# Two blocks on one core: the second block's first projections read their inputs before the norm, and its factor is applied at the eviction

## The chip, the cores and the metric

One NeuronCore of one Trainium2 chip runs the whole program in one launch. The metric is the device time in microseconds, given as the median of the runs. Five engines work in parallel, each through its own list of instructions, and wait for each other by semaphores: PE (TensorE: matmuls), ACT (ScalarE), DVE (VectorE), POOL (GpSimd) and SP (which only starts DMAs here).

## The reference, cut to what matters

Two transformer blocks follow one another on 512 tokens of width 1024. Block one has two layers and ends in a gated convolution MLP, a residual addition and an RMS norm with the gain `final_g`. Block two has two layers as well; each begins like this:

```
x = rms_norm(x_lat, final_g)                  # end of block one
for l in range(2):                            # block two
    h = rmsnorm(x, norm_mix_g[l])             # x * rsqrt(mean(x*x) + 1e-6) * g
    proj = h @ w_in[l]                        # 7328 columns, among them
    c_q, c_kv, k_pe, sb_q, sb_k, sb_v, r_q, r_k, r_v, r_g, gate_logits = split(proj)
    q  = rmsnorm(c_q, mla_q_norm_g[l])  @ mla_w_uq[l]
    kv = rmsnorm(c_kv, mla_kv_norm_g[l]) @ mla_w_ukv[l]
    ... three attention branches, gates, output projection ...
    x = x + square(relu(rmsnorm(x, norm_mlp_g[l]) @ w_up[l])) @ w_down[l]
```

The factor of an RMS norm is one number for each token. It commutes with a matmul over the width: `(x * g * s) @ W = ((x * g) @ W) * s`. "Latents" below are `c_q` (384 columns), `c_kv` (256) and `k_pe` (32); "values" are `sb_v` (512).

## The kernel before

**Layout.** Activations lie with the width on the 128 partitions: `X[:, k, 256:768]` (`lat(X, k)`) is slice k of 8 of the 512 tokens. The first 256 columns of each slice hold context rows in block one and are free later. Every weight is streamed in chunks; a chunk goes by DMA into one of three `raw` slots, ACT makes the rounded half `whi` of it (line 1392), DVE the rest `wlo` (line 2141), and PE multiplies three times for each slice: high by high, high by low, low by high (`lin`, line 608; `lin_pair`, line 647, alternates two chunks slice by slice; `lin_tok`, line 666, puts tokens on the partitions of the result). ACT and DVE split ahead by `LOOK` = 2 chunks, and a slot of `whi` or `wlo` comes free when PE has finished the chunk three before. An activation that feeds such a matmul is split in the same way, on ACT (`nh`) and DVE (`nl`); PE waits slice by slice for `nl`.

**Order.** All orders are written out by hand: each engine has one program (`pe_program`, `act_program`, and so on), and a wait holds up all that stands behind it on that engine. `Line.wait_ge` names events, `fence` names the place that all four engines have passed.

**The end of block one.** `conv_ffn(1, ...)` ends in eight output slices `ct`, each a chunk of 1024 rows and one of 384. DVE adds each to `X` (line 2432). `with_stats` squares the new slice on ACT (line 1443), POOL adds the squares of slices 0 to 6 (line 2919), and PE sums over the partitions with a matrix of ones in fp32 (lines 695 and 687, PSUM bank 6). Beside it a generator, `tables()`, makes the sine and cosine tables of block two, one step for each of the eight slices: the second table's sines come at the last slice. Then `in_place("fin1", ...)` scales all of `X` by the factor and `final_g` (lines 1826, 1828, 2612); ACT squares the eight new slices and PE sums them (lines 1101 to 1104); ACT makes the second factor (1416, 1419), DVE multiplies by gain and factor (2171), ACT and DVE split (1426, 2163), and the first pair of `w_in_2` starts. In the second layer of block two the same norm stands between the last `w_down_2` slice (additions in lines 2888 and 2890) and the pair, with the one sum that the MLP's slices have gathered.

**The latents and values.** P0 to P5 below are the six latent chunks of `w_in_2` (P0 and P1 are the pair, P5 holds `k_pe` four times), P6 to P9 the four chunks of the values (`lin_tok`, line 678). ACT evicts each latent (`evac_c`, line 1847) into `CQ` or `KR`; its squares are summed for the inner norms of `c_q` (after P3, bank 6) and `c_kv` (after P5, bank 7). The inner norm of `c_q` is made on ACT and DVE between P4 and P5, that of `c_kv` after P5. ACT evicts the values (line 1871). Later projections of `w_in_2` read the same `BH` and `BL`, first near the end of the MLA attention (`n` = 16).

**The model for the change that is already there.** The MLP of block two works in the way that the change gives to the latents: `u_high` and `u_low` (lines 2082 and 2863) split `x * norm_mlp` before the factor is known, beside the output projection; the pair of `w_up_2` follows at once, and the two sums come after it.

Of the kernel before, what the change touches and what calls it, by code (L numbers as in the profile page):

```python
# [307 lines left out]
def build(nc, A, out):  # L308
# [187 lines left out]
    POSI = at("posi", [128, TL], I32, oA)  # L496
    POSF, ANG, KKt, RR = ring("rt", 4, oA + 2 * KB)
    PRS = at("prs", [128, TL], F32, oT)[:, :]
    W = oR
    BNORM = (ring("brs", 1, W + 18 * KB), ring("btr", 3, W + 20 * KB))  # L500
# [52 lines left out]
    MLA_ITEMS = [(j, i) for j in range(4) for i in range(4)]  # L553

# [37 lines left out]
    def pe_program(q):  # L592
# [399 lines left out]
        def conv_ffn(i, segs, side, fill):  # L992
# [8 lines left out]
            for half in range(2):  # L1001
# [21 lines left out]
                if half:  # L1023
                    beside(fill)
                    with_stats(S, out_ct, True if i == 0 else None)
# [85 lines left out]
        for l in range(2):  # L1111
            q.note(f"end_mlp{l}", "pe")
            br = lambda k: [("nl", f"b{l}", k)]
# [14 lines left out]
            lin_tok("w_in_2", B, br, 4, TOK4)  # L1128
# [230 lines left out]
            for half in range(2):  # L1359
                for jj in range(16):  # L1360
# [5 lines left out]
                    lin("w_up_2", B, ur, ONE)  # L1366

# [3 lines left out]
                if half:  # L1371
                    with_stats(f"mlp{l}", down)
# [8 lines left out]
    def act_program(q):  # L1381
# [75 lines left out]
        def with_stats(S, step, ctx=False, high=None):  # L1457
# [10 lines left out]
            stats_square(S, 7, 7, srcs(7))  # L1468

# [207 lines left out]
        def conv_ffn(i, segs, mixer, side, fill):  # L1677
# [27 lines left out]
            for half in range(2):  # L1705
# [11 lines left out]
                def out_ct(ct):  # L1717
                    chunk("ffn_w_out")
                    chunk("ffn_w_out")
                    if half:  # L1720
                        next(side, None)

                if half:
                    with_stats(f"ffn{i}", out_ct, i == 0)
# [106 lines left out]
        in_place("fin1", "ffn1", fence("end_block1"))  # L1831
        for k in range(8):
            square("x2", k, 0, lat(X, k), k % 2, *sq_by[k % 2], ("x", "x2", k))
            sq_by[k % 2] = [("sqmm", "x2", k, 0)]

        for l in range(2):
            q.note(f"end_mlp{l}", "act")
            f = fence(f"end_mlp{l}")
            for _ in norm_high(f"b{l}", "mlp0" if l else "x2", 0, 8, lambda k: BH[:, k, :], BNORM, f, rbank=6 if l else 7):
                pass  # L1840
# [4 lines left out]
            def evac_c(i, ct):  # L1845
                q.wait_ge(("mm", i), *f)
                e.activation(CQ[:, ct, :] if ct < 5 else KR, PS[plan[i][6][0]], ACT.Copy).then_inc(q.did("ev", i, 0))
                q.note("cq", l, ct)

            pair = [chunk("w_in_2", n) for n in range(2)]  # L1850
            for ct, i in enumerate(pair):
                evac_c(i, ct)
            stats_square(f"q{l}", 0, 2, [(CQ[:, 0, :], [("cq", l, 0)])])
            for ct in range(2, 6):
                evac_c(chunk("w_in_2"), ct)
# [10 lines left out]
            f2 = fence(f"end_latent{l}")  # L1866
            for g in range(4):
                i = chunk("w_in_2")
            for ti, b in enumerate(plan[i][6]):
                q.wait_ge(("mm", i), *f)  # L1870
                e.activation(sv(ti), PS[b].rearrange("p (a k) -> p a k", a=2), ACT.Copy).then_inc(q.did("ev", i, ti))
                q.note("sv", l, ti)

# [54 lines left out]
            for n in range(16 + 4):  # L1928
# [185 lines left out]
            for half in range(2):  # L2114
# [3 lines left out]
                def down(ct):  # L2118
                    chunk("w_down_2")
                    chunk("w_down_2")  # L2120

                if half:
                    with_stats(f"mlp{l}", down)
# [8 lines left out]
    def dve_program(q):  # L2132
# [310 lines left out]

        def conv_ffn(i, segs, mixer, side, fill):
# [36 lines left out]
            for half in range(2):  # L2483
# [14 lines left out]
                for ct in range(8):  # L2498
# [4 lines left out]
                    if half:  # L2503
                        next(side, None)
                    else:
                        beside(fill, 2)
            if i == 0:
# [107 lines left out]
        in_place("fin1", "x2", "final_g")  # L2615
# [12 lines left out]
        for l in range(2):  # L2628
            q.note(f"end_mlp{l}", "dve")
            f = fence(f"end_mlp{l}")  # L2630
            for _ in norm_low(f"b{l}", None, 8, lambda k: (lat(X, k), []), lambda k: col("norm_mix", 8 * l + k),
# [611 lines left out]
```

## Time and profile before

| what | us |
|---|---|
| median of 3 runs | 3837.73 (3837.13 to 3845.9) |
| profiled execution, its own time | 3840.83 |
| span of its profile | 3839.0 |
| PE busy | 3713.3 (97%) |
| DVE busy | 1594.2 (42%) |
| ACT busy | 1389.4 (36%) |
| POOL busy | 243.1 (6%) |

Busy time says how long an engine worked, not whether anything waited for it. The span runs from the first to the last recorded instruction; 1.83 us of the execution lie around it. PE's mean granted clock was 0.988 of full speed.

### The profile page before, as it was taken

Reading aid. Unit: us, or ns where it says so; the run is one execution under the profiler, and the core shown is the slowest. Engines: PE = TensorE matmul, PEld = TensorE weight load, DVE = VectorE, ACT = ScalarE, POOL = GpSimd, SP = SyncE. Lnnn points to the kernel's source line nnn. Section 1 sums busy time; section 2 is a strip of 40 time slices with the busy share of each in tenths; the row PEclk is TensorE's granted clock in tenths of the full one; section 3 lists DMA queues with packets and bytes.
Section 4 is the critical chain, followed back from the end, with each engine's and each line's share of the span. In section 5 each row is a group of like instructions: output and inputs, shape, how many; then the busy total and the mean of one; then the engine's idle time right before and its main releaser. Section 6 shows DMA issues by size and latency. Waiting matters only on the chain.

```text
span 3839.0 us, 45566 instructions
## 1 busy us (share of the span) xinstructions
PE 3713.3 (97%) x19200; PEld 2998.7 (78%) x19200; DVE 1594.2 (42%) x2532; ACT 1389.4 (36%) x2265; POOL 243.1 (6%) x199
## 2 busy tenths in 40 slices
PE   7998899999999999999899999999999999999998
PEld 6887778888887977888676768888877676888887
DVE  3217635423434155545445443433334544343333
ACT  3235523212224155323346442342324544234232
POOL 1000010000000001000000001110110001112011
PEclk9999999999999999999999999999999999999999
DMA  6320122333312222233211123322221122332322
GB/s 231 110 83 2 37 74 89 115 122 126 113 62 87 66 67 75 94 94 95 89 57 50 66 74 100 102 93 99 96 90 57 56 72 69 97 104 93 99 94 83
DMA packets 108701, 333.98 MB, mean 87 GB/s; under 512 B 11472, under 2 KB 26704, under 8 KB 108368
## 3 DMA queue, kind: packets, MB, share of 16 engines
q1 hardware_dynamic: 108496, 331.06, 26.7%
q8 instruction: 151, 2.47, 0.3%
q14 instruction: 54, 0.44, 0.0%
HBM read 327.35 MB, written 2.10 MB: 86 GB/s over the span
## 4 chain that ended last, share of the span: by engine, by line
PE 93%; DVE 4%; ACT 2%; issue 1%; DMA 0%; POOL 0%; SPq 0%; DVEq 0%; ACTq 0%
PE ps L625 69%; PE ps L678 6%; PE ps L661 2%; PE ps L726 1%; PE ps L1230 1%; PE ps L880 1%; PE ps L1078 1%; PE ps L1066 1%; PE ps L1057 1%; PE ps L687 1%; PE ps L907 1%; PE ps L1233 1%; PE ps L1109 1%; PE ps L1274 1%; PE ps L1151 1%
## 5 line engine op out<-in xcount | busy, mean ns | idle before, releaser
L2141 DVE TENSOR_TENSOR wlo<-raw,whi 128x1024 fp32r<-128x1024 f32 (+3 forms) x547 | 618.6, 1132 | 887.3 <-ACT whi L1392 886.9
L1392 ACT ACTIVATE whi<-raw 128x1024 fp32r<-128x1024 f32 (+3 forms) x547 | 526.3, 964 | 795.8 <-PE ps L625 624.9
L625 PE MATMUL ps<-bh,whi 128*128 128x512 f32 x1248 | 494.8, 397 | 0.1
L625 PE MATMUL ps<-bh,wlo 128*128 128x512 f32 x1248 | 486.1, 389 | 0.0
L625 PE MATMUL ps<-bl,whi 128*128 128x512 f32 x1248 | 485.9, 389 | 0.0
L625 PE MATMUL ps<-ah,whi 128*128 128x512 f32 (+2 forms) x1424 | 423.3, 356 | 0.2 <-ACT gv L1537 0.2
L625 PE MATMUL ps<-al,whi 128*128 128x512 f32 (+2 forms) x1424 | 417.8, 352 | 0.0
L625 PE MATMUL ps<-ah,wlo 128*128 128x512 f32 (+2 forms) x1424 | 415.0, 350 | 0.0
L625 PEld LDWEIGHTS ps<-ah,whi 128*128 128x128 f32 x1424 | 240.0, 188 | 51.1 <-issue 18.3
L625 PEld LDWEIGHTS ps<-bh,whi 128*128 128x128 f32 x1248 | 234.3, 188 | 58.1 <-issue 7.6
L625 PEld LDWEIGHTS ps<-bl,whi 128*128 128x128 f32 x1248 | 234.4, 188 | 50.2 <-issue 2.9
L625 PEld LDWEIGHTS ps<-bh,wlo 128*128 128x128 f32 x1248 | 234.2, 188 | 49.5
L625 PEld LDWEIGHTS ps<-ah,wlo 128*128 128x128 f32 x1424 | 242.1, 188 | 31.7
L625 PEld LDWEIGHTS ps<-al,whi 128*128 128x128 f32 x1424 | 241.2, 188 | 29.3
L625 PE MATMUL ps<-uh,wlo 128*128 128x512 f32 x512 | 199.2, 389 | 0.0
L625 PE MATMUL ps<-uh,whi 128*128 128x512 f32 x512 | 199.2, 389 | 0.0
L625 PE MATMUL ps<-ul,whi 128*128 128x512 f32 x512 | 199.2, 389 | 0.0
L2919 POOL TENSOR_TENSOR sq<-sq,sq 128x512 f32<-128x512 f32 x50 | 77.1, 1542 | 1908.8 <-ACT sq L1443 1908.8
L2881 DVE TENSOR_TENSOR ul<-rl,uh 128x512 fp32r<-128x512 f32 x64 | 44.3, 692 | 204.3 <-ACT uh L2098 204.3
L625 PEld LDWEIGHTS ps<-uh,whi 128*128 128x128 f32 x512 | 96.1, 188 | 20.0
L625 PEld LDWEIGHTS ps<-ul,whi 128*128 128x128 f32 x512 | 96.1, 188 | 19.9
L625 PEld LDWEIGHTS ps<-uh,wlo 128*128 128x128 f32 x512 | 96.1, 188 | 19.9
(367 smaller groups left out, 5947.4 us busy)
## 6 DMA issues: line engine op xcount, KB each, us to landing
raw<-weights_d SPq DMA_DIRECT2D x447, 512.0 KB, 3.4
aw<-ada_d SPq DMA_DIRECT2D x96, 512.0 KB, 3.8
raw<-weights_d SPq DMA_DIRECT2D x48, 256.0 KB, 2.6
raw<-weights_d SPq DMA_DIRECT2D x44, 192.0 KB, 2.3
x<-nab_d SPq DMA_DIRECT2D x24, 256.0 KB, 2.8
x<-x_t_d SPq DMA_DIRECT2D x4, 1024.0 KB, 6.7
dt<-rtab_d SPq DMA_DIRECT2D x16, 256.0 KB, 2.8
out_d<-x SPq DMA_DIRECT2D x4, 512.0 KB, 3.1
```

Of the source, the lines that this page charges most:

```text
L625: m = e.matmul(p[:, 0:n], tiles(w, i)[:, k, :], xs[:, x0 + k, c0:c0 + n], start=pi == 0 and k == 0 and ti == 0, stop=i == job and k == kt ...
L661: m = e.matmul(p[:, 0:n], tiles(w, i)[:, k, :], xs[:, k, c0:c0 + n], start=k == 0 and ti == 0, stop=k == 7 and ti == 2, skip_group_check=True)
L678: m = e.matmul(p, xs[:, x0 + 2 * g + k, c0:c0 + 128], tiles(w, i)[:, k, :], start=g == 0 and k == 0 and pi == 0, stop=g == chunks - 1 and ...
L687: e.matmul(p[:, 0:n], ONES, SQ[buf][:, 0:n], start=start, stop=stop, skip_group_check=True).then_inc(q.did("sqmm", S, k, r))
L726: mm = e.matmul(p[at32:at32 + 32, 0:256], CS[:, at2:at2 + 32], side_slot(m)[0][:, k, 256 * half:256 * half + 256], start=g == 0, stop=g == ...
L880: m = e.matmul(p[:, 128 * c:128 * c + 128], XK[l % 2][:, cc], XQ[l % 2][:, cc], start=True, stop=True, skip_group_check=True)
L907: m = e.matmul(p[:, 128 * c:128 * c + 128], l_, r_, start=j == 0, stop=j == len(terms) - 1, skip_group_check=True)
L1057: m = e.matmul(ps[b][:, o:o + 256], NQ[r, j, 128 * i:128 * i + 128], NK[r, j, c0:c0 + 256], start=True, stop=True, skip_group_check=True)
L1392: e.activation(flat(WHI, j), raw(j), ACT.Copy).then_inc(q.did("hi", j))
L2141: e.tensor_tensor(flat(WLO, j), raw(j), flat(WHI, j).bitcast(F32), ALU.subtract).then_inc(q.did("lo", j))
L2881: e.tensor_tensor(UL[:, jj, :], RL[m % 3], UH[:, jj, :].bitcast(F32), ALU.subtract).then_inc(q.did("ul", l, half, jj))
L2919: e.tensor_tensor(SQ[0], SQ[0], SQ[1], ALU.add).then_inc(q.did("sqacc", S, k))
```

## The change

Block two's `BH` and `BL` get two contents in each layer. First they hold the split of `x * gain` without a norm's factor (events `bu`): in the first layer the gain is `final_g * norm_mix` (the small tile `FG`) on the x in front of block one's last norm. They are made beside the last output slices (`entry_high` on ACT, `entry_low` on DVE). P0 to P9 read them. The latents are then evicted by DVE with the factor (`evac_c`), and the values by ACT with the factor turned onto the partitions (`BRC`: four fp32 matmuls with 2 columns behind P3, one copy). Second, while PE works on P6 to P9 and in the first steps of the attention, `b_low`, `b_rest` and `b_high` make the normed contents (events `b`) for the projections that come later.

In the first layer two factors are needed. The squares of `x * final_g` are summed in the same pass (`SQF` in the free columns of `X`, POOL additions `sqacc fin`, two fp32 matmuls into bank 7), and the second factor is computed from that sum and the first factor (`entry_rms`). The scaling of `X` itself (`scaled`) stands between the evictions of P2 to P5. The table steps are spread as 1, 1, 2, 2, 1, 1, 0, 0 over the eight slices, and the tables' scratch tiles move.

```diff
@@ layout
+    PRS, BRS0 = ring("prs", 2, W + 26 * KB)
+    RS2 = ring("rs2_", 1, oX0 + 46 * KB)[0]
+    MS = ring("ms", 2, W + 22 * KB)
+    SQF = [X[:, 2 * i:2 * i + 2, 0:256] for i in range(2)]
+    BTR = ring("bt", 2, oA + 44 * KB)
...
+    TABLE_STEPS = (1, 1, 2, 2, 1, 1, 0, 0)
@@ pe_program
-        for k in range(8):
-            if k == 0:
-                bank(7, ("ln", "x2", 0))
-            square_sum("x2", k, TL, PS[7], k == 0, k == 7, 0, k % 2)
...
-            lin_pair(["w_in_2", "w_in_2"], B, br, ONE)
-            stats_add(f"q{l}", 0, None)
+            lin_pair(["w_in_2", "w_in_2"], B, bu, ONE)
+            stats_add("mlp0" if l else "ffn1", 7, 7)
+            if l == 0:
+                p = bank(7, ("ms",))
+                q.wait_ge(("sqacc", "fin", 6))
+                e.matmul(halved(p), ONES, SQF[0], start=True, stop=False, skip_group_check=True)
+                q.wait_ge(("sqf", 7))
+                e.matmul(halved(p), ONES, SQF[1], start=False, stop=True, skip_group_check=True).then_inc(q.did("sqfmm"))
             for ct in range(2, 6):
-                lin("w_in_2", B, br, ONE)
+                lin("w_in_2", B, bu, ONE)
+                if ct == 3:
+                    p = bank(7, ("rc", l))
+                    q.wait_ge(("br", l))
+                    for t in range(4):
+                        m = e.matmul(p[:, 2 * t:2 * t + 2], entry_rs(l)[:, 128 * t:128 * t + 128], IDENT[:, 0:2], start=True, stop=True,
+                                     skip_group_check=True)
+                    m.then_inc(q.did("rcmm", l))
...
-            lin_tok("w_in_2", B, br, 4, TOK4)
+            lin_tok("w_in_2", B, bu, 4, TOK4)
@@ act_program
+        def entry_high(l, S, k, free):
+
+            q.wait_ge(("x", S, k, 0), ("fg",), *free)
+            e.activation(BH[:, k, :], lat(X, k), ACT.Copy, scale=entry_gain(l, k)).then_inc(q.did("nh", f"bu{l}", k))
+            if l == 0:
+                q.wait_ge(*([("sqacc", "fin", k - 1)] if k > 1 else []))
+                e.activation(SQF[k > 0], halved(lat(X, k)), ACT.Square, scale=col("final_g", k)).then_inc(q.did("sqf", k))
...
-                        next(side, None)
+                        for _ in range(TABLE_STEPS[ct]):
+                            next(side, None)
+                        if i and ct:
+                            entry_high(0, "ffn1", ct - 1, fence("end_tabs"))
...
-        in_place("fin1", "ffn1", fence("end_block1"))
-        for k in range(8):
-            square("x2", k, 0, lat(X, k), k % 2, *sq_by[k % 2], ("x", "x2", k))
-            sq_by[k % 2] = [("sqmm", "x2", k, 0)]
+        def entry_rms(l):
+
+            S = "mlp0" if l else "ffn1"
+            rs = RS2 if l else PRS
+            ln_exp()
+            q.wait_ge(("sqmm", S, 7, 0), *f)
+            e.activation(rs, PS[6], ACT.Ln, scale=1.0 / D, bias=col("eps")).then_inc(q.did("ln", S, 0))
+            q.wait_ge(("ln", S, 0))
+            if l == 0:
+                e.activation(MS[0], rs, ACT.Exp, scale=-1.0).then_inc(q.did("ms0"))
+            e.activation(rs, rs, ACT.Exp, scale=-0.5).then_inc(q.did("br", 1) if l else q.did("prs"))
+            if l == 0:
+                q.wait_ge(("ms",))
+                e.activation(RS2, MS[1], ACT.Ln, scale=1.0 / D, bias=col("eps")).then_inc(q.did("br0"))
+                q.wait_ge(("br0",))
+                e.activation(RS2, RS2, ACT.Exp, scale=-0.5).then_inc(q.did("br1"))
...
-            for ct, i in enumerate(pair):
-                evac_c(i, ct)
+            for n in range(2):
+                chunk("w_in_2", n)
+            entry_rms(l)
...
+            def b_high(i, k):
+                q.wait_ge(("nt", f"b{l}", k), ("mm", i))
+                e.activation(BH[:, k, :], BTR[k % 2], ACT.Copy).then_inc(q.did("nh", f"b{l}", k))
...
+                if g:
+                    b_high(i - 1, 2 * g - 2)
+                    b_high(i - 1, 2 * g - 1)
...
+            b_high(i, 6)
...
+                if n == 2:
+                    b_high(sv_last, 7)
...
+                    if half and l == 0 and ct:
+                        entry_high(1, "mlp0", ct - 1, [("upped", 0)])
@@ dve_program
+        def entry_low(l, k):
+            q.wait_ge(("nh", f"bu{l}", k))
+            e.scalar_tensor_tensor(BL[:, k, :], lat(X, k), entry_gain(l, k), BH[:, k, :].bitcast(F32), ALU.mult, ALU.subtract
+                                   ).then_inc(q.did("nl", f"bu{l}", k))
...
-        in_place("fin1", "x2", "final_g")
...
+            def evac_c(i, ct):
+                q.wait_ge(("mm", i), ("br", l), *f)
+                e.tensor_tensor(CQ[:, ct, :] if ct < 5 else KR, PS[plan[i][6][0]], entry_rs(l), ALU.mult).then_inc(q.did("ev", i, 0))
+                q.note("cq", l, ct)
...
+                e.tensor_tensor(MS[1], PS[7], MS[0], ALU.mult).then_inc(q.did("ms"))
+                q.wait_ge(("br1",), ("prs",))
+                e.tensor_tensor(BRS0, RS2, PRS, ALU.mult).then_inc(q.did("br", 0))
...
             for ct in range(2, 6):
-                chunk("w_in_2")
+                evac_c(chunk("w_in_2"), ct)
+                if l == 0:
+                    scaled(2 * ct - 4)
+                    scaled(2 * ct - 3)
+                if ct == 3:
+                    q.wait_ge(("rcmm", l))
+                    e.tensor_copy(BRC[:, :], PS[7][:, 0:8]).then_inc(q.did("rc", l))
...
+            def b_low(k):
+
+                q.wait_ge(("br", l), *([] if l else [("x", "x2", k)]), *([("nl", f"b{l}", k - 2)] if k >= 2 else []))
+                e.scalar_tensor_tensor(BTR[k % 2], lat(X, k), col("norm_mix", 8 * l + k), RS2, ALU.mult, ALU.mult
+                                       ).then_inc(q.did("nt", f"b{l}", k))
+                if k:
+                    b_rest(k - 1)
...
+                if n == 1:
+                    b_low(7)
+                if n == 2:
+                    b_rest(7)
@@ pool_program
+                if fin:
+                    q.wait_ge(("sqf", k), ("sqf", 0), *([("sqacc", "fin", k - 1)] if k > 1 else []))
+                    e.tensor_tensor(SQF[0], SQF[0], SQF[1], ALU.add).then_inc(q.did("sqacc", "fin", k))
```

## Rows read from the trace of the kernel before

**Rows 1.** Page, part 4: shares of the chain that ended last, by engine.

```profile
PE 93%; DVE 4%; ACT 2%; issue 1%; DMA 0%; POOL 0%; SPq 0%; DVEq 0%; ACTq 0%
```

**Rows 2.** Waits of PE: who waited for whom, total us, times, longest.

```profile
PE ps L695 <- POOL sq L2919: 7.5, 1, 7.5
PE ps L661 <- DVE bl L2163: 7.4, 2, 3.7
```

**Rows 3.** Chain of waits, 1880 to 2060: start us, us, what.

```profile
1895.04 0.66 DVE x L2432
...
1899.57 0.72 ACT tab L1816
...
1921.65 12.78 PE ps L661 x48
1934.44 10.89 PE ps L625 x48
...
1947.65 5.50 PE ps L625 x24
...
1961.03 1.12 PE ps L687 x2
1962.16 21.79 PE ps L678 x96
```

**Rows 4.** PE timeline, last projection matmul of block one: start us, us, instruction.

```profile
1894.28 0.39 PE L625 MATMUL ps<-f1yh,wlo 128*128 128x512 f32 x1
```

**Rows 5.** Windows: us, busy per engine (x instructions), granted clock, DMA share, GB/s.

```profile
1921.60:1934.30 12.70, 12.65 (x49) 10.27 (x50) 9.41 (x14) 5.25 (x8) 0.00 (x0) 0.87 0.13 41
...
2876.20:2890.10 13.90, 13.84 (x49) 11.26 (x50) 9.42 (x14) 5.33 (x8) 0.00 (x0) 0.79 0.12 38
```

**Rows 6.** Chain of waits, 2830 to 3010.

```profile
2869.23 0.70 DVE utmp L2888
...
2876.26 13.88 PE ps L661 x48
...
2903.35 5.50 PE ps L625 x24
...
2917.86 21.79 PE ps L678 x96
```

**Rows 7.** PE timeline, first statistics sum after the first layer's MLP.

```profile
2869.04 1.02 PE L695 MATMUL ps<-sq,fix 128*128 128x512 f32 x2
```

**Rows 8.** Chain of waits, 2490 to 2545: from output projection into up projection.

```profile
2518.91 0.70 DVE x L2625
...
2519.66 10.50 PE ps L661 x45
2530.15 0.86 PE ps L695 x2
```

**Rows 9.** PE timeline: two 4-column matmuls on a 128x128 weight (four records).

```profile
689.98 0.50 PE L737 MATMUL ps<-sel,rows 128*128 128x4 f32 x4
```

**Rows 10.** DVE timeline, inner norm of the first layer.

```profile
1955.57 1.42 DVE L2171 SCALAR_TENSOR_TENSOR btr<-cq,small,brs 128x512 f32<-128x512 f32 x2 [6.89 <-ACT brs L1419]
...
1960.01 1.22 DVE L2141 TENSOR_TENSOR wlo<-raw,whi 128x1024 fp32r<-128x1024 f32 x1 [0.26 <-ACT whi L1392]
```

**Rows 11.** ACT timeline, end of that norm; [] is idle before, and releaser.

```profile
1958.94 1.04 ACT L1392 ACTIVATE whi<-raw 128x1024 fp32r<-128x1024 f32 x1
1959.89 0.58 ACT L1847 ACTIVATE kr<-ps 128x512 f32<-128x512 f32 x1
```

**Rows 12.** POOL timeline, a statistics addition inside the MLP.

```profile
2843.75 1.81 POOL L2919 TENSOR_TENSOR sq<-sq,sq 128x512 f32<-128x512 f32 x1 [9.07 <-ACT sq L1443]
```

**Rows 13.** DVE timeline, attention of the second layer.

```profile
2959.99 0.68 DVE L2669 COPY kn<-ps 128x512 f32<-128x512 f32 x1
...
2969.02 0.69 DVE L2664 TENSOR_TENSOR qr<-qr,tm 128x512 f32<-128x512 f32 x1 [0.66 <-POOL qr L2964]
```

**Rows 14.** Windows: attention stage of the first layer.

```profile
2015.60:2060.00 44.40, 41.09 (x289) 24.86 (x290) 25.95 (x89) 27.47 (x79) 0.00 (x0) 1.00 0.14 48
```

More of the change, by code:

```diff
@@ L1024, in conv_ffn @@
                     beside(fill)
-                    with_stats(S, out_ct, True if i == 0 else None)
+                    with_stats(S, out_ct, True if i == 0 else None, last=i == 0)
                 else:
@@ L1366, in pe_program @@
                     lin("w_up_2", B, ur, ONE)
+                if half:
+                    q.note("upped", l)
                 def down(ct):
@@ L1371, in pe_program @@
                 if half:
-                    with_stats(f"mlp{l}", down)
+                    with_stats(f"mlp{l}", down, last=l == 1)
                 else:
@@ L1838, in act_program @@
             f = fence(f"end_mlp{l}")
-            for _ in norm_high(f"b{l}", "mlp0" if l else "x2", 0, 8, lambda k: BH[:, k, :], BNORM, f, rbank=6 if l else 7):
-                pass
             q.note(f"end_bnorm{l}", "act")
             f = fence(f"end_bnorm{l}")
[L1845 to L1850, printed above, removed]
-            for ct, i in enumerate(pair):
-                evac_c(i, ct)
+            for n in range(2):
+                chunk("w_in_2", n)
+            entry_rms(l)
             stats_square(f"q{l}", 0, 2, [(CQ[:, 0, :], [("cq", l, 0)])])
             for ct in range(2, 6):
-                evac_c(chunk("w_in_2"), ct)
+                chunk("w_in_2")
                 if ct < 4:
@@ L2503, in conv_ffn @@
                     if half:
-                        next(side, None)
+                        for _ in range(TABLE_STEPS[ct]):
+                            next(side, None)
+                        if i and ct:
+                            entry_low(0, ct - 1)
                     else:
                         beside(fill, 2)
+            if i == 1:
+                entry_low(0, 7)
             if i == 0:
@@ L2652, in dve_program, with b_rest @@
             f2 = fence(f"end_latent{l}")
-            for _ in range(4):
+            def b_low(k):
[4 more added lines that the diff above has]
+                    b_rest(k - 1)
+            def b_rest(k):
+                q.wait_ge(("nh", f"b{l}", k))
+                e.tensor_tensor(BL[:, k, :], BTR[k % 2], BH[:, k, :].bitcast(F32), ALU.subtract
+                                ).then_inc(q.did("nl", f"b{l}", k))
+            for g in range(4):
                 chunk("w_in_2")
+                if g:
+                    b_low(2 * g - 2)
+                    b_low(2 * g - 1)
+            b_low(6)
             rotate(6, ("kr", l), KR, COSM, SINM, TMP[1], *f2)
@@ L2906, in dve_program @@
                     add_down(f"mlp{l}" if half else f"mlph{l}", ct, chunk("w_down_2"), 8 * half + ct)
+                    if half and l == 0 and ct:
+                        entry_low(1, ct - 1)
+            if l == 0:
+                entry_low(1, 7)
         q.note("end_mlp2", "dve")
@@ L2956, in pool_program @@
         q.note("end_tabs", "pool")
-        square_sums("ffn1", 7)
+        square_sums("ffn1", 7, True)
         q.note("end_block1", "pool")
```

43 lines of the change are left out of this document (29 added, 14 removed).

## The prediction

> **What bounds the kernel now.** I read the chain of waits by engine first: PE holds 93% of it, DVE and ACT 6% [rows 1]. So time can be gained in two ways: fewer or faster matmuls, or gaps of PE closed. Next I read PE's waits, to find the gaps. Among the longest single ones stand 7.5 us for POOL's addition of squares and two waits of 3.7 us for the split `bl` [rows 2]; both lie at the two places that this change touches. The chain in order of time then shows what fills them. At the end of block one the last slice is added at 1895.04, but the second table's sines run until 1900.29 in front of the square, and then come POOL, sums, the scaling, eight more squares and sums, and the norm; the pair starts at 1921.65 [rows 3]. PE's last projection matmul starts at 1894.28 [rows 4]. Matmuls of 512 columns follow each other at 10.89/48 = 0.227 us [rows 3], so PE was free at 1894.5: 27.1 us to the pair. The windows add something the waits do not show: the pair runs at a granted clock of 0.87 in the first layer and 0.79 in the second [rows 5], so part of it is at the lower level (1.2 GHz) after the gap. It takes 12.8 and 13.9 us [rows 3, 6] where the same pattern without a gap, the pair of `w_up_2`, takes 10.50 for its last 45 matmuls [rows 8].
>
> **The entry, first layer.** The new pair needs no factor, only `bu` slice by slice. Slice 6 is split behind the last `hi`, slice 7 right after the last addition; with 0.7 us each on ACT and DVE, slice 7 is ready near 1897.1. PE wants it after seven of eight steps of 6 matmuls, 9.5 us after the start: no wait. P1 writes the PSUM bank that the last slice leaves, so its first matmul waits for that addition, which ends at 1895.70. That is the situation of [rows 8]: DVE ends at 2519.61, PE goes on 0.05 later and reaches the sums 10.49 us after that. Here: 1895.75 + 10.49 = 1906.2. Then four sums of 0.86 [rows 8] (two of them new), 3.4 us: P2 starts at 1909.7 instead of 1934.44 [rows 3]. Step: 24.7 us, of which eight sums and the sines are the larger part. What the entry adds before 1894 is hidden: for each slice ACT gets two instructions of 0.7, DVE one, POOL a second addition of at most 1.81 [rows 12], and PE works about 7.5 us on a slice (33 matmuls of 0.227). The table steps put at most six DVE instructions of 0.7 into one slice, 4.2, beside a split of 1.22 [rows 10] and one of a third of its width, an addition and the new split of 0.7 each: at most 7.3, under 7.5. The last additions on POOL end near 1898, 8 us before PE's sums want them. SP moves no DMA across another.
>
> **P2 and P3, first layer.** The `hi` of P3 stands on ACT behind `entry_rms` and the square of the first latent. From the end of the sums: DVE 0.7, ACT 0.7 and 0.64, DVE 0.7 for the product, eviction 0.7, square 0.64, `hi` 1.05, `lo` 1.23 [rows 3, 10, 11]: 6.4 us, to 1916.1. PE finishes P2 after 5.4 and wants `lo` after two more matmuls, at 1915.6: 0.5 lost. P3 ends at 1909.7 + 10.9 + 0.5 = 1921.1. Then the four turning matmuls. Two of such a kind took 0.50 [rows 9], so I take 1.0 (0.7 to 2). With two sums (1.7) P4 starts at 1923.8; before, P3 ended at 1945.33 and P4 started at 1947.65, since the square stood behind an eviction [rows 3]. The lead is 23.8.
>
> **P4 to P6, first layer.** P4 and P5 need 10.9: 1934.7. The sum for `c_kv` waits for a square that stands on ACT behind the inner norm. DVE starts this norm now after evicting P4 (1929.3 + 0.7) and two scalings (1.42, the pair of [rows 10]): 1931.4. From there to the end of the next `hi` it took 1955.57 to 1959.98 [rows 10, 11], 4.4 us; the eviction of 0.58 that followed [rows 11] is gone from ACT, the square needs 0.64: 1936.5. With a sum of 1.13 P6 starts at 1937.6 instead of 1962.16 [rows 3]: **24.6 us** for the first layer.
>
> **Second layer.** PE is free at 2869.04 [rows 7]; DVE's first half of the addition, which frees the bank, ends at 2869.93 [rows 6]; the pair ends at 2869.97 + 10.49 = 2880.5, two sums: P2 at 2882.2 instead of 2890.14 (2876.26 + 13.88) [rows 6]. Here one factor is enough, 4.95 us from the sums to `lo` of P3, under P2's 5.4: no stall. P3 ends at 2893.1, P4 starts 2.7 later at 2895.8 (before 2903.35), P5 ends at 2906.7. No scalings here: eviction at 2901.2 + 0.7, norm 4.4, square 0.64 gives 2907.0, the sum 2908.1 instead of 2917.86 [rows 6]: **9.8 us**. Some 3 us of it are clock.
>
> **P6 to P9 and the attention.** The second split costs DVE 8 x 1.4 and ACT 8 x 0.65, seven eighths of it under 21.8 us of PE [rows 3], where both engines have few other things to do; each step waits only for a chunk that PE has left. The rest falls into the attention: DVE 1.4 behind the copy at 2959.99 and 0.7 a step later, ACT 0.65. Bounds: nothing, or all of it, 2.8 a layer. The next copy, softmax and evictions move by about 1.0, but then DVE stands 0.66 waiting for POOL at 2969.02 [rows 13], which POOL's own start fixes; most is taken up there. I take 0.5 a layer. A late DVE or ACT here stops PE through the attention's transposes, since scores, exponentials and turns wait for each other.
>
> **Sum.** 24.6 + 9.8 - 1.0 = 33.4 us off the profiled execution's 3840.8 (span 3839.0): 3807.4. That execution lies 3.1 above the median; against 3837.7 it gives **3804**. Terms with bounds: turning matmuls 1.4 to 4 in all, attention 0 to 5.6, stall of P3 0 to 2, the clock's part of the pairs (at most 1.9 and 3.0 us, 12.8 and 13.9 against 10.9) gone only if the gaps are.
>
> **Rivals.** (1) The attention passes on all that is put into it: 5.6 instead of 1.0. For it: ACT, DVE and PE hand over there step by step. Against it: the wait of [rows 13]. Time 3809. (2) DVE becomes the bound of the latents: it now holds evictions, splits of weights, scalings and inner norms in one queue. Where an eviction stands behind a `lo` (1.23) and two scalings (1.42), up to 2.7 is added at P3 and at P5 in the first layer and 1.2 twice in the second: 8 us, 3812. Against it: DVE was idle 6.89 us before the inner norm [rows 10]. (3) The first slices' work beside block one does not stay hidden, and the sums wait for POOL; the 8 us of slack would have to vanish first and then the gain of the first layer with it: to 3829 if all 24.6 go. Nothing in the rows speaks for it. (4) The other side: the small gaps that remain lower the clock. In the attention PE is busy 41.1 of 44.4 us at clock 1.00 [rows 14], although it has many short gaps; if the delays there made the grant fall to 1.2 GHz, these 41 us would take 41 more in each layer: 3804 + 82 = 3886. It decides for slower from 33 us of full-rate work at the lower level. Against it: P4 and P5 end near 1947.65 + 10.89 = 1958.5, PE stands until 1961.03, and P6 to P9 still run 96 matmuls in 21.79, full speed [rows 3].
>
> The Trainium skill (TensorE: Matmul & The Clock Gate, section A second HAM failure mode: psum-queue depth-cycling) describes a kernel whose clock swings between its two levels because of short idle moments between groups of matmuls. By that rule rival 4 would be the outcome; the trace of this kernel does not agree with it in that stage, with its clock of 1.00.
>
> **How the numbers follow.** Forecast 67%, rival 1 14%, rival 2 12%, rival 3 3%, rival 4 4%. A change within 0.3% (11.5 us) could not be told from none. Rivals 1 and 2 are still faster by more than that, so faster has 95%; rival 3 in full and a small share of rival 4 give the same, 2%; rival 4 gives slower, 3%. The forecast alone spans 3800 to 3808. The range takes in rivals 1 and 2 and, downward, attention and turning at nothing and the noise of a few us that the three runs show: 3797 to 3814.
>
> **What would show it.** Pair right behind the last output slice, at clock 1.00, with one short wait for the last addition; four sums together, then P2; no wait for POOL; about 0.5 us of waiting at P3 in the first layer and none in the second; P6 about 24.6 and 33.9 us earlier than before; the start of the stick-breaking stage with 0.5 less of lead each. The prediction is wrong if PE waits inside the pair, if P6's lead is more than 3 us off, if the attention grows by over 1.5 us a layer, or if the granted clock falls anywhere after 1800 us.

## The result, and the profile after

The changed kernel takes 3812.26 us (median of 5 runs, 3810.64 to 3820.69), the kernel before 3842.2 in the same session: a ratio of 0.993, with a 95% interval of 0.9918 to 0.9942. The forecast was 3804, with a range of 3797 to 3814. Set against the profiled executions, the basis of the forecast's sum, 28.6 us went (3840.83 to 3812.26) where 33.4 had been expected. The direction, the places and most terms hold; 4.8 us are missing. The time lies inside the range, but not for the range's reasons: its upper end stood for rivals 1 and 2, and neither came.

The page's part 4, the counterpart of [rows 1]: POOL is no longer on the chain, and PE is still the bound.

```profile
PE 92%; DVE 4%; ACT 2%; issue 1%; DMA 0%; SPq 0%; POOL 0%; DVEq 0%; ACTq 0%
```

PE's waits from 1800 to 1960 us. The 7.5 and 3.7 us of [rows 2] are gone, and four small waits have come. The first two lines belong to block one's last slices, which the forecast took as hidden (0.5 us of the first is P3's); L644 is the projection helper that was L625, L680 the pair that was L661.

```profile
PE ps L644 <- DVE wlo L2200: 2.0, 2, 1.5
PE ps L644 <- ACT whi L1421: 0.7, 1, 0.7
PE ps L706 <- ACT sq L1472: 0.7, 1, 0.7
PE ps L680 <- DVE x L2491: 0.4, 1, 0.4
```

The chain of waits through the first layer's entry (start us, us, what), which answers to [rows 3].

```profile
1897.69 10.50 PE ps L680 x45
1908.20 0.86 PE ps L714 x2
...
1911.67 0.70 DVE ms L2715
...
1916.88 1.24 DVE wlo L2200
...
1918.16 5.28 PE ps L644 x22
1923.44 0.79 PE ps L1147 x8
...
1926.05 5.50 PE ps L644 x24
...
1939.62 21.80 PE ps L697 x96
```

The pair's last 45 matmuls take 10.50, as in [rows 8]. Four sums of 0.86 follow, P2, a wait at P3 (PE stands 0.53 us for `wlo`) whose chain runs DVE, ACT, DVE, ACT, DVE from 1911.67 to 1918.12, the turning matmuls (0.79 for the four of them, eight records), and P6 starts at 1939.62 instead of 1962.16 [rows 3]. The second layer's entry, against [rows 6]:

```profile
2848.36 10.50 PE ps L680 x45
2858.86 0.86 PE ps L714 x2
...
2860.58 10.93 PE ps L644 x48
2871.51 0.79 PE ps L1147 x8
...
2885.05 0.86 PE ps L714 x2
...
2886.76 21.81 PE ps L697 x96
```

P2 and P3, and then P4 and P5, run there without a gap (10.93 us each pair of chunks). Windows of the two pairs and of the end of the second layer's attention (us; busy PE, PEld, DVE, ACT, POOL; granted clock; DMA share; GB/s), against [rows 5]:

```profile
1897.60:1908.20 10.60, 10.51 (x46) 8.73 (x47) 4.17 (x4) 4.25 (x5) 2.40 (x2) 1.00 0.31 99
...
2848.30:2858.80 10.50, 10.44 (x46) 8.66 (x47) 3.34 (x5) 2.19 (x3) 0.00 (x0) 1.00 0.15 50
2982.00:2988.00 6.00, 4.70 (x17) 3.98 (x18) 3.14 (x9) 3.44 (x9) 0.00 (x0) 0.72 0.00 0
```

Both pairs now run at clock 1.00 (0.87 and 0.79 before). The last row is new and was not foreseen: a fall to the lower level (1.2 GHz) behind a wait for the turned scores (the transposed attention scores, which ACT copies out of PSUM as `mpt`). The PE timeline shows the wait, the chain its price:

```profile
2983.30 1.35 PE L1189 MATMUL ps<-fix,mp 128*128 128x128 f32 x6 [1.66 <-ACT mpt L1955]
```

```profile
2981.47 1.52 ACT mp L1948 x4
2983.30 1.35 PE ps L1189 x6
2984.66 6.59 PE ps L644 x24
```

The kernel before has the same place at 3011.63, with the same wait but without a fall, so the same PE work took 0.87 + 5.45 instead of 1.35 + 6.59:

```profile
3011.63 1.52 ACT mp L1893 x4
...
3013.47 0.87 PE ps L1162 x6
3014.35 5.45 PE ps L625 x24
```

```profile
3013.47 0.87 PE L1162 MATMUL ps<-fix,mp 128*128 128x128 f32 x6 [1.66 <-ACT mpt L1900]
```

**Where 33.4 became 28.6.** The account, from differences between the marks of the two traces (rounded, so the measured column adds up to 28.7):

| stretch | forecast | measured |
|---|---|---|
| before block one's last slices | 0 | +0.8 |
| block one's last slices, to the start of the pair | 0 | -2.7 |
| pair to P6, first layer | 24.6 | 24.5 |
| attention, first layer | -0.5 | -0.9 |
| second layer's entry to P6 | 9.8 | 9.5 |
| attention, second layer | -0.5 | -0.9 |
| granted clock at 2983 us | 0 | -1.6 |
| sum | 33.4 | 28.6 |

The 0.8 stands before the change does anything: it is luck of the two executions, and without it 5.6 us would be missing. Three things are to be explained: the slices, the attention, the clock.

**The slices.** The ACT timeline at slice 5 (brackets: idle before, and releaser):

```profile
1882.26 0.63 ACT L1852 ACTIVATE tab<-rt 128x512 f32<-128x512 f32 x1 [4.76 <-DVE rt L2673]
...
1884.22 0.71 ACT L1502 ACTIVATE bh<-x,fg 128x512 fp32r<-128x512 f32 x1
...
1885.96 1.46 ACT L1421 ACTIVATE whi<-raw 128x1024 fp32r<-128x1024 f32 x2
```

ACT stands 4.76 us until DVE ends its table step of this slice; its three instructions for the tables (two of them sines) and three of the entry and its squares follow, and only then the weights' high half that PE needs next. The DVE timeline behind it, and POOL's:

```profile
1887.04 2.18 DVE L2200 TENSOR_TENSOR wlo<-raw,whi 128x1024 fp32r<-128x1024 f32 x1 [1.33 <-ACT whi L1421]
```

```profile
1885.62 1.28 POOL L3037 TENSOR_TENSOR x<-x 128x512 f32<-128x512 f32 x1 [11.56 <-ACT x L1505]
1886.86 1.28 POOL L3039 TENSOR_TENSOR sq<-sq,sq 128x512 f32<-128x512 f32 x1
1888.72 1.64 POOL L3037 TENSOR_TENSOR x<-x 128x512 f32<-128x512 f32 x1 [0.59 <-ACT x L1505]
```

The subtraction of 1.22 [rows 10] takes 2.18. POOL's addition runs from 1886.86 to 1888.14; 1888.14 + 1.22 = 1889.36, and DVE's instruction ends at 1889.22, as if it had stood until POOL was done. The same is seen in the attention: two scalings of the scores, 0.75 us for both before, take 1.76 beside POOL's rotation of 1989.42 to 1990.86, which begins during the first of them. DVE timelines, before and then changed:

```profile
2011.32 0.75 DVE L2687 TENSOR_SCALAR mp<-mp,tiny 128x384 f32<-128x384 f32 x2
```

```profile
1989.31 1.76 DVE L2796 TENSOR_SCALAR mp<-mp,tiny 128x384 f32<-128x384 f32 x2
```

The Trainium skill (SBUF — State Buffer, section Who interferes with whom) says that VectorE and GpSimd share a pair of SBUF ports, and that a VectorE instruction in a two-port mode, or one with two SBUF inputs beside a GpSimd instruction that reads SBUF, and that of GpSimd shut each other out for the whole of the one that began first. The subtraction's trace agrees with it to 0.14 us. For the scalings the second one, 0.33 us before (0.75 less the first one's 0.42), would end at 1990.86 + 0.33 = 1991.19 and ends at 1991.07; in which mode they run no row shows.

### The profile page after: what moved, and what is told of

It reads as the page before. It is cut to its first block, busy times and chain, and to the rows that moved or that the text cites. A ratio compares the mean times of both kernels' runs of the same rounds, so it can differ in the third digit from the quotient of the medians.

```text
span 3810.5 us, 45608 instructions
## 1 busy us (share of the span) xinstructions
PE 3704.3 (97%) x19204; PEld 2998.9 (79%) x19204; DVE 1623.9 (43%) x2565; ACT 1393.8 (37%) x2270; POOL 250.8 (7%) x205
## 4 chain that ended last, share of the span: by engine, by line
PE 92%; DVE 4%; ACT 2%; issue 1%; DMA 0%; SPq 0%; POOL 0%; DVEq 0%; ACTq 0%
PE ps L644 69%; PE ps L697 6%; PE ps L680 2%; PE ps L745 1%; PE ps L1257 1%; PE ps L899 1%; PE ps L1097 1%; PE ps L1076 1%; PE ps L1085 1%; PE ps L926 1%; PE ps L1260 1%; PE ps L858 1%; PE ps L1301 1%; PE ps L1315 1%; PE ps L706 1%
## 5 line engine op out<-in xcount | busy, mean ns | idle before, releaser
L644 PE MATMUL ps<-bh,whi 128*128 128x512 f32 x1248 | 496.8, 398 | 0.1
L644 PE MATMUL ps<-bh,wlo 128*128 128x512 f32 x1248 | 487.1, 390 | 0.5 <-DVE wlo L2200 0.5
L644 PE MATMUL ps<-bl,whi 128*128 128x512 f32 x1248 | 486.9, 390 | 0.0
L644 PE MATMUL ps<-ah,whi 128*128 128x512 f32 (+2 forms) x1424 | 423.8, 357 | 0.2 <-ACT gv L1574 0.2
L644 PE MATMUL ps<-al,whi 128*128 128x512 f32 (+2 forms) x1424 | 418.1, 353 | 0.0
L644 PE MATMUL ps<-ah,wlo 128*128 128x512 f32 (+2 forms) x1424 | 415.5, 351 | 0.0
L644 PEld LDWEIGHTS ps<-bh,whi 128*128 128x128 f32 x1248 | 234.9, 188 | 58.6 <-issue 8.0
L644 PEld LDWEIGHTS ps<-ah,whi 128*128 128x128 f32 x1424 | 240.1, 188 | 51.1 <-issue 18.7
L644 PEld LDWEIGHTS ps<-bh,wlo 128*128 128x128 f32 x1248 | 234.7, 188 | 50.5 <-DVE wlo L2200 1.0
L644 PEld LDWEIGHTS ps<-bl,whi 128*128 128x128 f32 x1248 | 234.9, 188 | 50.3 <-issue 3.3
L644 PEld LDWEIGHTS ps<-ah,wlo 128*128 128x128 f32 x1424 | 242.2, 188 | 31.4
L644 PEld LDWEIGHTS ps<-al,whi 128*128 128x128 f32 x1424 | 241.3, 188 | 29.2
L644 PE MATMUL ps<-uh,whi 128*128 128x512 f32 x512 | 199.4, 389 | 0.0
L644 PE MATMUL ps<-uh,wlo 128*128 128x512 f32 x512 | 199.4, 389 | 0.0
L644 PE MATMUL ps<-ul,whi 128*128 128x512 f32 x512 | 199.4, 389 | 0.0
L644 PEld LDWEIGHTS ps<-uh,wlo 128*128 128x128 f32 x512 | 96.2, 188 | 20.0
L644 PEld LDWEIGHTS ps<-uh,whi 128*128 128x128 f32 x512 | 96.2, 188 | 19.9
L644 PEld LDWEIGHTS ps<-ul,whi 128*128 128x128 f32 x512 | 96.2, 188 | 19.8
```

What stands on the lines that cost most here:

```text
L644: m = e.matmul(p[:, 0:n], tiles(w, i)[:, k, :], xs[:, x0 + k, c0:c0 + n], start=pi == 0 and k == 0 and ti == 0, stop=i == job and k == kt ...
```

## The experiments

Leads are compared at marks of the chain, so that differences upstream of block one's end (the pair of matmul chunks near 1533 us starts between 1530.48 and 1536.38, up to 5.9 us apart) do not count. **A** runs from the end of that pair to the end of the first layer's entry pair, **B** from there to the end of the second layer's entry pair, **C** from there to the end of the pair in front of `w_up_2` of the second layer (3457.31 in the changed kernel). A granted-clock fall inside a stretch is named. A, B and C come from one profiled execution of each kernel. The ratio is to the kernel before of the same session, whose median was 3841.45, 3841.22 or 3840.23; all the intervals but that of the last row lie almost on one another, so between those kernels the times decide nothing, and the marks have to.

| kernel | A | B | C | median us, ratio |
|---|---|---|---|---|
| changed (three executions; time of the second) | 362.5 | 950.7 | 598.5, fall at 2983 | 3811.82, 0.9924 [0.9912, 0.9936] |
| sines | 359.8 | 950.8 | 596.9 | 3810.73, 0.9920 [0.9906, 0.9933] |
| no final sums | 361.8 | 950.7 | 596.9 | 3810.52, 0.9920 [0.9906, 0.9935] |
| both of these | 359.7 | 950.7 | 596.9 | 3810.61, 0.9916 [0.9900, 0.9931] |
| slice 7 | 362.5 | 949.7 | 596.0 | 3811.33, 0.9920 [0.9905, 0.9935] |
| high half first | 362.5 | 951.2, fall at 2033 | 598.3, fall at 2982 | 3812.01, 0.9926 [0.9911, 0.9941] |
| all three orders | 359.8 | 948.9 | 597.6, fall at 2978 | 3804.79, 0.9904 [0.9891, 0.9918] |

The forecast's own A was 1906.2 - 1546.5 = 359.7.

**The changed kernel again**, in two of the three sessions.

> The changed kernel again, beside the others. Both theories: the same profile as before, 28 to 29 us under the kernel before, if the short fall of the clock in the second layer's attention (2983 to 2987 us) comes again; without it 1.6 us less. Theory: that fall belongs to the execution and not to the kernel, so it may be missing here or stand elsewhere. Rival: it comes at the same place each time.

> The changed kernel again, beside the three reorderings together. Both theories: a ratio of 0.992 to 0.993. For the clock: if the short fall at 2983 us behind the 1.66 us wait for the turned scores belongs to this kernel, it stands here again; if it is a matter of the moment, as its absence with the sines exchanged and without the additions on POOL says, it may stand or not.

Measured: 3811.82 (3809.53 to 3814.98) and 3812.48 (3811.16 to 3814.75), ratios 0.9924 and 0.9925 [0.9912, 0.9937]. All three profiled executions have the fall at 2983 us, as the rival said; my theory, that it belongs to the execution, is not borne out here, and not excluded either (what speaks for it stands at the end of the account). The changed kernel's median lies 29.9, 29.6 and 27.8 us under that of the kernel before in the result's session and these two.

**Each layer alone.** The new entry is kept in one layer; the other has the old norm, the old evictions and the unpaired sums.

```
+    FU = (0,)          # and (1,) in the other kernel
+    TABLE_STEPS = (1, 1, 2, 2, 1, 1, 0, 0) if 0 in FU else (1,) * 8
-                        if i and ct:
+                        if i and ct and 0 in FU:
                             entry_high(0, "ffn1", ct - 1, ...)
...
+                if l not in FU: return      # the eviction with its factor
```

> Only the first layer has the change, the second keeps its norm. Theory (the gains of the two layers add up): the second layer's pair keeps its gap of 7 us, and of the 28.6 us the first layer alone brings 21 to 22 less 0.9 in its attention, so about 20.5 to 21.5 us under the kernel before. Rival (the layers share something, the clock for one): clearly more or less than that.

> Only the second layer has the change; block one's end, its tables and the first layer are as before. Theory: 9.5 us less up to P6 of the second layer, 0.9 given back in the attention: 8 to 9 us under the kernel before. Rival (no part of the second layer's gain is its own): under 5 us.

Measured: 3820.83 (ratio 0.9946 [0.9932, 0.9959]) and 3834.99 (0.9984 [0.9975, 0.9993]); the spans fall from 3839.0 to 3817.9 and to 3832.3, 21.1 and 6.7. Their sum, 27.8, lies near the change's 28.5, but each has terms of the clock that the other lacks. The slices' waits stand in the first kernel as in the full change (1.5 and 0.7 us) and not in the second. The second is worth less than expected for one visible reason: its entry brings the full 9.5, the attention takes 0.9, and a fall of the clock at 3005 us 1.7 more (the kernel's window 3000 to 3015):

```profile
3000.00:3015.00 15.00, 13.33 (x72) 9.48 (x69) 5.89 (x17) 7.05 (x19) 0.00 (x0) 0.89 0.11 36
```

The first has such a fall too (1.7 us, from 2991 us on), starts 0.7 earlier, and the second layer's pair, which it leaves as it was, took 12.61 instead of 13.88 us:

```profile
2854.76 12.61 PE ps L681 x48
```

So 21.1 is 20.8 of the first layer's own, and 0.7 and 1.3 more, less 1.7. Without the clock and the start the layers give 20.8 and 8.6, together 29.4; the change gives 28.5 - 0.8 + 1.6 = 29.3. They add up, but the 21.1 inside the expected 20.5 to 21.5 is in part luck.

**Sines a slice later.** ACT's sines of slice 5 move to slice 6; DVE's table steps stay.

```
+    SINE_STEPS = (1, 1, 2, 2, 1, 0, 1, 0)
-                        for _ in range(TABLE_STEPS[ct]):
+                        for _ in range(SINE_STEPS[ct]):
```

> ACT takes the second table's sines one slice later (its steps 1,1,2,2,1,0,1,0, DVE's as they are). Theory (ACT stands 4.8 us for DVE's last table step with the weight splits behind it): the wait disappears, PE's waits for whi and wlo in block one's last slices fall from 2.7 us to under 0.5, the whole is 2 to 2.7 us faster than the changed kernel. Rival (POOL's doubled additions stretch DVE's splits from 1.2 to 1.9 us, and that alone makes PE wait): 1.5 us or more of the waits stay.

Measured: A falls by 2.7 us, all that the slices had lost. The only waits of PE left up to the first P6 are these (0.5 is P3's):

```profile
PE ps L707 <- ACT sq L1473: 0.7, 1, 0.7
PE ps L645 <- DVE wlo L2201: 0.5, 1, 0.5
PE ps L681 <- DVE x L2492: 0.4, 1, 0.4
```

ACT's timeline tells how: the high half that stood at 1885.96 behind the sines is now done at 1882.18, right behind the squares. The smaller one (384 rows) waits for its buffer until 1887.48, and the sines come behind it, when DVE's step has ended (1886.57).

```profile
1882.18 1.04 ACT L1422 ACTIVATE whi<-raw 128x1024 fp32r<-128x1024 f32 x1
1887.48 0.53 ACT L1422 ACTIVATE whi<-raw 128x384 fp32r<-128x384 f32 x1 [4.25 <-PE ps L645]
1887.91 0.62 ACT L1853 ACTIVATE tab<-rt 128x512 f32<-128x512 f32 x1
```

The median moves by 1.1 only, less than its uncertainty: in the profiled execution the pair of 1534 us ran at a lower mean clock and cost 1.4 more (13.99 against 12.64), upstream of anything changed. The two other kernels with the sines moved have the same there (14.02 and 13.82), and none of the other ten executions (12.48 to 12.77). Whether it belongs to these kernels or to the moment no run shows.

**No final sums.** POOL's six additions of the squares of the final input are left out, so that statistic is a part of the squares only; it tells DVE's share in the slices from ACT's.

```
-                q.wait_ge(*([("sqacc", "fin", k - 1)] if k > 1 else []))        # ACT
+                q.wait_ge(*([("sqf", k - 1)] if k > 1 else []))
...
-                    q.wait_ge(("sqf", k), ("sqf", 0), *([("sqacc", "fin", k - 1)] if k > 1 else []))
-                    e.tensor_tensor(SQF[0], SQF[0], SQF[1], ALU.add).then_inc(...)
+                    q.wait_ge(("sqf", k), ("sqf", 0))           # POOL
```

> POOL's six additions of the squares of x * final_g are left out; the second statistics sum then covers only two slices. All else is as in the changed kernel. Theory (ACT's wait for the table step is the cause in block one's last slices): DVE's weight splits go back from 1.9 to about 1.2 us each, which saves PE 1.2 of its 2.7 us of waits at most, since ACT's late whi stays; 1 to 1.5 us are left. Rival (POOL's additions are the cause): the waits go under 0.3 us.

ACT's squares no longer wait for POOL's addition either; in slice 5 of the changed kernel ACT had not stood for it.

Measured: A falls by 0.7, where at most 1.2 was expected. DVE's two low halves take 1.97 together instead of 3.75 (DVE timeline of this kernel), and the longest wait of PE for one falls from 1.5 to 0.8; the wait of 0.7 for ACT stays.

```profile
1886.97 1.97 DVE L2200 TENSOR_TENSOR wlo<-raw,whi 128x1024 fp32r<-128x1024 f32 x2 [1.33 <-ACT whi L1421]
```

So without the additions 0.7 of the slices' 2.7 goes and 2.0 stays, and with ACT in time all 2.7 goes although POOL adds as before (one low half still takes 2.28 there). ACT's order makes the wait; the meeting of DVE and POOL lengthens it by 0.7 and costs nothing by itself, as the two together confirm:

**Both of these:** the sines a slice later, and no final sums.

> The changed kernel with the sines exchanged as before, and POOL's six additions of the final input's squares left out (the sum takes a part of the squares only). Theory (the sines' order makes the wait in slice 5, and what is left, 0.5 us for DVE's low half, comes from DVE and POOL using SBUF at once): PE has no wait over 0.2 us for a weight half between 1800 and 1896 us, DVE's low halves there take 1.22 us each, and the stretch of block one's slices is 348.0 us long as with the sines alone or up to 0.5 shorter. Rival (DVE is slow there for another reason, its own queue of table steps): the 0.5 stays, and low halves of 1.9 us stand beside the table steps though POOL adds less.

Measured: no wait of PE between 1800 and 1896 us, and an A of 359.7, as with the sines alone. My expectation had put the 0.5 us that is left into the slices; it is P3's. The longest low half is 1.53 us instead of 2.28, so they did not all return to 1.22: one addition of POOL is still beside it.

**Slice 7 of the second split ahead of the attention.**

```
+            b_high(sv_last, 7)            # ACT: ahead of the values' evictions
...
-                if n == 2:
-                    b_high(sv_last, 7)
```

and on DVE `b_low(7)` and `b_rest(7)` around the value projection's chunk instead of after the first and second chunk of the heads.

> The last slice of the second split (b_low, b_rest, b_high of slice 7) stands before the value projection of the attention, where DVE and ACT stood idle for over 4 us, and no longer in the steps n = 1 and 2. Theory: the 0.94 us that each layer's attention lost comes back, 1.9 us in all, and DVE's two scalings of 128x384 beside POOL's rotation go from 1.76 back to 0.75. Rival (the loss comes from the scaled eviction of the values or from slice 6): no change.

Measured: B falls by 0.9 and C (against the kernels without a fall) by 0.9, the 0.9 that each attention had lost. The DVE timeline, before with the change and then here, shows the exchange: in place of the split of slice 7 ahead of the scores DVE has its 0.66 of waiting for POOL back, and the scalings, begun before POOL's rotation (1986.63), take 0.75 again. The run shows that the 0.9 hangs on where slice 7 stands. That the slower scalings carry it is read from the timelines: the move also takes some 2 us of DVE's work out of these steps, and no run parts the two.

```profile
1987.29 0.68 DVE L2755 TENSOR_TENSOR bl<-bt,bh 128x512 fp32r<-128x512 f32 x1
```

```profile
1986.01 0.75 DVE L2795 TENSOR_SCALAR mp<-mp,tiny 128x384 f32<-128x384 f32 x2
1988.01 0.69 DVE L2772 TENSOR_TENSOR qr<-qr,tm 128x512 f32<-128x512 f32 x1 [0.66 <-POOL qr L3081]
```

**High half first.** The high and the low half of P3's weights are made ahead of the entry's factor, on ACT and DVE.

```
+            high_half()
             entry_rms(l)
...
+            low_half()
             q.wait_ge(("sqfmm",), ("ms0",))
```

> ACT and DVE split P3's weights ahead of entry_rms. Theory: PE's wait of about 0.65 us inside P3 of the first layer goes, the second layer does not change: 0.6 us faster in the trace, under what the times can tell. Rival (P3 waits for the eviction of the first latent): the wait stays.

Measured: P2 and P3 run without a gap:

```profile
1910.23 10.89 PE ps L644 x48
1921.12 0.79 PE ps L1147 x8
```

10.89 instead of 11.80 (1911.64 to 1923.44). The 0.9 gained did not reach the end: a fall of the clock came at 2033 us, in the last third of the first layer's attention, and B is longer by 0.5. Among the kernels with the change it is the only one with a fall there. Window 2030 to 2038:

```profile
2030.00:2038.00 8.00, 6.33 (x30) 4.54 (x29) 4.99 (x12) 4.45 (x10) 0.00 (x0) 0.79 0.00 0
```

**Filler ahead of the pairs of the kernel before.** Three and four matmuls with no use, in front of the first and second layer's pair, while PE waits anyway.

```
+            p = bank(5)
+            q.wait_ge(("c2",))
+            for _ in range(3 + l):
+                e.matmul(p, ONES, C2[:, 0:512], start=True, stop=True, ...)
```

> The kernel before with three (first layer) and four (second) fp32 matmuls of 512 columns on constants into an idle bank, in the gap ahead of the pair; their results are used nowhere. Theory (the pair was slow by the clock alone): the pairs go from 12.8 and 13.9 us to about 11, 4 to 5 us less in all, so about a seventh of the change's gain is clock. Rival (the split delivers a slice every 1.27 us and that paces the pair): they stay at 12.8 and 13.9 and the whole stays or gets slower.

Measured: the pairs take 11.16 and 11.14 instead of 12.78 and 13.88, at clock 1.00; that is the clock's part in the change's gain, 1.6 and 2.7 us. The rival, that the split paces the pair, is left with the 0.3 us over 10.89.

```profile
1921.65 11.16 PE ps L661 x48
...
2876.19 11.14 PE ps L661 x48
```

The span falls by 2.8 and not 4.3, since here a fall appears that the kernel before did not have, at 2056 us (window 2054 to 2061: 0.76): the place of the fall at 2033 us of the kernel above, behind the same wait. The time, 3838.22 against 3841.22, gives 0.9991 [0.9982, 1.0001]: not told apart from no change.

**All three orders together:** sines, slice 7, high half first, on the changed kernel.

> The changed kernel with three reorderings together: sine steps of block one's slices 5 and 6 exchanged on ACT (one step leaves slice 5 for slice 6), the first latents' high and low split ahead of the entry's factor, and slice 7 of the second split ahead of the value projection's chunk. Theory (three separate delays that add): the stretch from the pair of the stick-breaking block's end to the next pair is 2.7 us shorter than in the changed kernel, P0 to P6 0.9 shorter in the first layer and nothing in the second, each attention 0.93 shorter: 5.5 in all, so a median near 3806 and a ratio of 0.991 to the kernel before. Rival (the granted clock takes back what the gaps give): one or more short falls to 1.2 GHz of 1.7 us each stand after 1800 us, and the median stays within 2 us of the changed kernel's, 3810 to 3812.

Measured: 3804.79 (3803.41 to 3806.7) beside 3812.48 for the changed kernel in the same session. Between the marks it is 5.4 us shorter (A 2.7, B 1.8, C 0.9), with the fall at the end of the second attention still there; the theory of separate delays said 5.5. The medians differ by 7.7, of which the marks explain 5.4; the rest is within the spread of single runs. Of the expectation's rival the fall came, but not its bound: the median left 3810 to 3812. PE's waits from 1800 to 1960 are down to two, 0.7 for the square ahead of P6 and 0.4 for the last addition.

It is the fastest of the kernels run.

## Why the prediction was right or wrong

The step that failed first of all is the one that took block one's last slices as hidden; smaller misses are the attention, P3's wait and the clock.

- **Bound and places: right.** The gaps of PE at the two entries were the gain. From the start of the pair to P6 the first layer gives 24.5 of 24.6, the second 9.5 of 9.8. Within them: sums and pair as worked out (15.2 us from P0's first matmul to P2), turning matmuls 0.8 for 1.0. P3 lost 0.9 for 0.5 (11.80 against 10.89 without it), of which 0.53 is recorded as a wait. In the second layer two sums follow P5 (1.7 us) where the forecast had a single one of 1.13 behind the square; that is its 0.3.
- **The clock's part: right in size.** "Some 3 us of it are clock" in the second layer: 2.7, by the filler.
- **"What the entry adds before 1894 is hidden": wrong, 2.7 us.** The step summed the work of one slice per engine (7.3 under 7.5) and found room. The room is there, as the sines' version shows, but the order isn't: ACT, a queue in order, waited 4.76 us for a table step of DVE with work behind it that PE needed first; with three of ACT's instructions moved one slice on, all 2.7 came back. The order of ACT's queue, and where it waits for DVE, had to be followed instruction by instruction. Rival 3 named the place, not the mechanism (POOL's sums were in time), and took its chance at 3%.
- **The same step, second half: POOL was priced on its own engine only.** POOL's additions doubled next to DVE's splits; DVE's 1.22 became 2.18. That is 0.7 of the 2.7, and only where ACT is late.
- **Attention, 0.5 a layer: wrong by 0.4 each.** The 0.66 of waiting for POOL [rows 13] was to take up most of the delay. It did go, but DVE then met POOL's rotation with two scalings (1.76 for 0.75), as much again. 0.9 was inside the bounds of nothing to 2.8. Moving slice 7 got 0.9 back twice: its place is the cause, and that it acts through the scalings is the timelines' reading.
- **"The prediction is wrong if the granted clock falls anywhere after 1800 us": it does, 1.6 us.** Rival 4 was right that the clock may fall behind a small wait, and wrong in size by far: one short fall, not the whole stage. Its ground for nothing, [rows 14], is a mean over one execution; the trace of before shows the same 1.66 us wait twice without a fall. The other signs of being wrong did not come: PE has no wait inside the pair but the one for the last addition, P6's leads were 22.5 and 31.1 us for 24.6 and 33.9 (under 3 off), and the attention grew by 0.9 a layer, the clock aside.
- **The base.** The 3804 came off a median of before of 3837.7, from three runs; with two more beside the result the median is 3842.2. The same sum on that gives 3842.2 - 33.4 = 3808.8, so of the 8.3 us between 3804 and 3812.3 some 4.5 come from the base and the rest from the terms above.
- **The range: held by luck.** 3797 to 3814 took in 3812.3, but its upper end was made for an attention that passes on 5.6 us (it passed on 1.8) and for a DVE that bounds the latents (P4 and P5 ran in 10.9 us in both layers, and P3 lost 0.9 where up to 2.7 was at stake). What filled it instead were the base and the slices.

What stays open is when such a wait is followed by a fall. Every one of the 13 profiled executions has the 1.66 us wait in the last third of both attentions, 26 times in all. Nine of them were followed by a fall. In the second attention it was seven: the changed kernel three times, each layer alone, high half first, all three orders. In the first it was two: high half first, and the kernel before with filler. The changed kernel's three agree, which speaks for something in the kernel. Against it speaks a place that no edit touches: at 1092 and again at 1380 us five executions have a fall (each layer alone, sines, both of these, filler) and eight do not, with the same waits of PE in front of the first of them (1.7 us in two). The kernel before and the same kernel with filler run the same instructions there, and their clock from 1090 to 1100 us is 1.00 and 0.83. No run isolates what decides it.

## What to carry to other kernels

Work that fits into a stretch by its sum is hidden only if each in-order queue reaches what the bound engine needs next before it waits for another engine: write down that order, and put what the bound engine waits for ahead of every cross-engine wait. Work given to POOL can have a price on DVE: a DVE subtraction that began inside a POOL addition ended here as if it had run after it, so count such a pair one after the other. A gain of a few us from closed gaps can be masked by a fall of the clock elsewhere, whether or not the change caused it, so it is read between marks in the trace, and whether it stays is told by many runs.

## What the runs showed of the hardware

- A DVE subtraction of 128x1024 took 1.22 us alone and 2.18 to 2.28 when a POOL addition had begun before it; two scalings of 128x384 took 1.76 instead of 0.75.
- The same PE wait of 1.66 us (last third of each attention) was followed by the lower clock level in 9 of 26 cases; at 2983 us PE's work behind it then cost 1.6 us more. At 1092 us the level fell in five executions and not in eight, with unchanged instructions.
- Three or four matmuls of filler in front of a pair that started after a gap kept the pair at clock 1.00 (11.16 and 11.14 us), where it had run at 0.87 and 0.79 (12.78 and 13.88 us).
